# A state space stage: running sums of the heads as rows through HBM instead of by TensorE

## The reference

```
Q = 128                                  # chunk; 256 tokens are 2 chunks
G, Hg, P, N = 4, 8, 64, 128              # 4 groups of 8 heads, head width 64, state width 128
dt = softplus(dt_raw + dt_bias)
cs = cumsum(dt * A, axis=positions of the chunk)          # one running sum per head and chunk
xdt = xs * dt
seg = cs[i] - cs[j]                                       # i, j positions of one chunk
decay = exp(where(i >= j, seg, -inf))
CB = einsum("ign,jgn->ijg", Cm, Bm)
y_diag = einsum("ijgh,jghp->ighp", CB * decay, xdt)
states = einsum("jgn,jgh,jghp->ghpn", Bm, exp(cs[last] - cs), xdt)
y_off = einsum("ign,ghpn,igh->ighp", Cm, state of the chunk before, exp(cs))
y = y_diag + y_off + xs * D_skip
out = rmsnorm(y * silu(z)) @ out_w
```

## Time and profile before

| what | value |
|---|---|
| median of three runs | 3217.51 us |
| the profiled execution | 3220.12 us, its span 3218.3 us |
| PE busy | 3141.3 us (98%) |
| VectorE busy | 1262.0 us (39%) |
| ScalarE busy | 704.8 us (22%) |
| GpSimd busy | 278.2 us (9%) |
| chain that ended last | PE 84%, DMA 9%, VectorE 4% |
| granted clock of the whole span | 0.993 |
| the stage of the change | slots 0 to 31, about 48 to 203 us |

### The profile page before, as it was taken

The page is one execution under the profiler, slowest core; times in us unless marked ns, Lnnn a source line. Parts: engine busy times, 40 slices in busy tenths (PEclk is TensorE's granted clock), DMA queues, the critical chain, the costliest instruction groups (busy, mean ns, idle before and its releaser), DMA issues.

```text
span 3218.3 us, 44517 instructions
## 1 busy us (share of the span) xinstructions
PE 3141.3 (98%) x18164; PEld 2444.3 (76%) x18164; DVE 1262.0 (39%) x2669; ACT 704.8 (22%) x1251; POOL 278.2 (9%) x231
## 2 busy tenths in 40 slices
PE   8999999998999999999999999999999999999998
PEld 7888899987899888998789988888554455545444
DVE  4532177463378544753357543431211111111111
ACT  3531121252221043102211123420111111111111
POOL 0120011061011110001100013200000000000000
PEclk9999999999999999999999999999999999999999
DMA  5233244432344433443244433235799999999996
GB/s 226 105 131 131 101 174 164 164 131 92 118 159 160 157 126 119 171 171 144 105 153 170 171 144 130 75 127 209 318 428 428 428 428 428 429 428 429 428 429 260
DMA packets 71250, 715.30 MB, mean 222 GB/s; under 512 B 7969, under 2 KB 7969, under 8 KB 9153
## 3 DMA queue, kind: packets, MB, share of 16 engines
q1 hardware_dynamic: 70416, 710.06, 55.9%
q0 software_dynamic: 688, 3.15, 0.3%
HBM read 712.13 MB, written 1.05 MB: 222 GB/s over the span
## 4 chain that ended last, share of the span: by engine, by line
PE 84%; DMA 9%; DVE 4%; ACT 1%; issue 1%; POOL 0%; SPq 0%; DVEq 0%; POOLq 0%; ACTq 0%
PE bank L285 30%; PE bank L2375 11%; PE bank L3448 10%; DMA weight_ring<-in_experts 9%; PE bank L304 8%; PE bank L1374 8%; PE bank L3479 5%; PE bank L3433 2%; PE bank L3425 2%; PE bank L2673 1%; DVE residual L1119 1%; PE bank L1226 0%; PE bank L1206 0%; PE bank L344 0%; PE bank L758 0%
## 5 line engine op out<-in xcount | busy, mean ns | idle before, releaser
L285 PE MATMUL bank<-normed_residual,weight_ring 128*128 128x256 f32 x2592 | 576.1, 380 | 0.0
L285 PEld LDWEIGHTS bank<-normed_residual,weight_ring 128*128 128x128 f32 x2592 | 487.7, 190 | 71.8 <-issue 8.5
L285 PE MATMUL bank<-arena,weight_ring 128*128 128x256 f32 x1368 | 304.2, 383 | 4.7 <-ACT arena L1733 3.9
L285 PEld LDWEIGHTS bank<-arena,weight_ring 128*128 128x128 f32 x1368 | 262.0, 192 | 41.8 <-issue 4.8
L3532 DVE TENSOR_TENSOR arena<-bank,arena 128x512 f32<-128x512 f32 x32 | 22.1, 691 | 615.9 <-PE bank L3448 615.9
L3448 PE MATMUL bank<-weight_ring,arena 128*64 128x512 f32 x1024 | 227.6, 593 | 3.1 <-DMA weight_ring<-in_experts 3.1
L3448 PE MATMUL bank<-arena 128*64 128x512 f32 x1024 | 226.9, 596 | 2.3 <-DVE arena L3526 2.3
L304 PE MATMUL bank<-gained_residual,weight_ring 128*128 128x256 f32 x896 | 205.7, 390 | 23.9 <-DVE gained_residual L378 12.0
L3479 PE MATMUL bank<-weight_ring,arena 128*64 128x512 f32 x992 | 219.7, 595 | 0.0
L304 PEld LDWEIGHTS bank<-gained_residual,weight_ring 128*128 128x128 f32 x896 | 174.9, 196 | 51.4 <-DVE gained_residual L378 14.0
L3448 PEld LDWEIGHTS bank<-weight_ring,arena 128*64 128x64 f32 x1024 | 72.6, 137 | 152.7 <-issue 139.0
(11 more groups left out here) (446 smaller groups left out, 4253.9 us busy)
## 6 DMA issues: line engine op xcount, KB each, us to landing
weight_ring<-in_stream SPq DMA_DIRECT2D x290, 1024.0 KB, 4.8
weight_ring<-in_experts SPq DMA_DIRECT2D x126, 2048.0 KB, 18.6
arena<-in_experts SPq DMA_DIRECT2D x66, 2048.0 KB, 18.7
residual<-in_x SPq DMA_DIRECT2D x1, 1024.0 KB, 4.9
arena<-in_mem POOLq DMA_DIRECT2D x1, 1024.0 KB, 5.3
out<-gained_residual SPq DMA_DIRECT2D x4, 256.0 KB, 2.8
constants<-in_con SPq DMA_DIRECT2D x1, 612.5 KB, 7.3
vectors<-in_vec SPq DMA_DIRECT2D x1, 548.5 KB, 6.2
```

The source lines that it names most:

```text
L285: mm = nc.tensor.matmul(PB[b][:, m * T:m * T + T], l, r, start=(kc == 0), stop=(kc == chunks - 1))
```

## The change

The running sums of all 32 heads as rows are made once: two more matmuls in front of slot 0, with DTA as the weights and `upto` moving, give 32 partitions (one per head) by 128 positions for each chunk, in bank 4. ScalarE copies them to the arena (`CS_ROWS`). GpSimd issues a DMA that writes them to a scratch tensor in HBM (32 KB), waits for it, and then issues loads that read the rows of four heads and both chunks, 4 KB, into each of the 128 partitions, 512 KB per load. There are eight such loads, one per pair of batches, into two buffers in turn: two at once, each later one after the L1017 of the pair that used the buffer. VectorE's subtraction and ScalarE's ECS read these buffers instead of banks 4 and 5. L758 is gone with its waits, and the head outputs go to banks 4 and 5, so bank 6 holds states alone. The wait for the states moves to the head outputs of chunk 1, for their own group.

A few semaphores of later blocks are merged (`lam_in` and `lb_ready` into `exp_in`, `lam_exp` and `lbs` into `exp_out`), with the counts of the waits adapted; they make no difference in what waits for what.

```diff
+        CS_ROWS = A[0:32, 72, :]
+        def seg_rows(n):
+            return flat(92 + 4 * (n % 2), 4).rearrange("p (c t) -> p c t", c=2)
+        def seg_source(i):
+            return seg_rows(i // 2)[:, i % 2, :]
         def y_bank(j):
-            return PB[7 - j % 2]
+            return PB[4 + j % 2]
@@ ssm_slot_pe
             if s in CR_AT:
-                pe.wait_ge(sem["dte_in"], 1)
-                if i >= 2:
-                    pe.wait_ge(sem["seg_ready"], i - 1)
-                if i >= 3:
-                    pe.wait_ge(sem["ecs_ready"], (i - 1) // 2)
-                for k in range(4):
-                    h = g * HPG + half * 4 + k
-                    mm = nc.tensor.matmul(PB[4 + i % 2][:, k * P:k * P + P], DTA[:, c, h:h + 1].broadcast_to([P, P]),
-                                          upto, start=True, stop=True)
-                mm.then_inc(sem["cr_mm"], 1)
                 if i % 4 == 0:
                     pe.wait_ge(sem["xde_ready"], g + 1)
...
                     if g:
-                        pe.wait_ge(sem["y_ready"], 4 * g - 2)
+                        pe.wait_ge(sem["st_ready"], g)
@@ head outputs
-                pe.wait_ge(sem["st_ready"], before(CR_AT[0:16:4], s + 1))
                 if c:
+                    pe.wait_ge(sem["st_ready"], g + 1)
                     pe.wait_ge(sem["cp_ready"], j // 2 + 1)
@@ ssm_pe, in front of slot 0
+            for c in range(2):
+                mm = nc.tensor.matmul(PB[4][0:32, c * P:c * P + P], DTA[:, c, :], upto, start=True, stop=True)
+            mm.then_inc(sem["cs_mm"], 1)
@@ ssm_act, after silu_act(act, 2)
+            act.wait_ge(sem["cs_mm"], 1)
+            nc.scalar.activation(CS_ROWS, PB[4][0:32, 0:T], ACT.Identity)
@@ ssm_slot_act
-                    nc.scalar.activation(flat(ECS, 2), PB[4 + i % 2][:, :], ACT.Exp).then_inc(sem["ecs_ready"], 1)
+                    nc.scalar.activation(flat(ECS, 2), seg_source(i), ACT.Exp).then_inc(sem["ecs_ready"], 1)
@@ ssm_slot_dve
-                dve.wait_ge(sem["cr_mm"], i + 1)
+                if c == 0:
+                    dve.wait_ge(sem[f"seg_in{i // 2 % 2}"], 16 * (i // 4 + 1))
@@ ssm_pool
+        def rows_pool(pool, n):
+            src = io["rows"][:, 4 * n:4 * n + 4, :].rearrange("c h t -> c (h t)").unsqueeze(0).broadcast_to([P, 2, 512])
+            pool.dma_start(seg_rows(n), src).then_inc(sem[f"seg_in{n % 2}"], 16)
...
             pool.wait_ge(sem["dte_ready"], 1)
+            pool.dma_start(io["rows"].rearrange("c h t -> h c t"),
+                           CS_ROWS.rearrange("h (c t) -> h c t", c=2)).then_inc(sem["cs_sent"], 16)
+            pool.wait_ge(sem["cs_sent"], 16)
+            for n in range(2):
+                rows_pool(pool, n)
...
+                    if n + 2 < 8:
+                        rows_pool(pool, n + 2)
```

More of the change, by code:

```diff
@@ L182 @@
 cb_mm cbm_ready btok_ready dte_in dte_ready xt_mm xdt_ready xde_ready st_mm st_ready
-cr_mm seg_ready ecs_ready e_ready g_ready cp_ready y_mm y_ready
+cs_sent seg_in0 seg_in1 seg_ready ecs_ready e_ready g_ready cp_ready y_mm y_ready
 sc_mm s_read smax_ready exp_done p_ready pt_mm pts_ready o_mm o_evac
@@ L187 @@
 z_mm zabs_ready zln_ready spm_ready rs_mm rs_read sw_ready so_mm so_evac
-lam_in lam_mm lam_exp lam_ready
+exp_in lam_mm exp_out lam_ready
 hn_sq hn_stat hn_var hn_std hn_out
 kf_ready b_ready d_ready lev_exp q_side k_side lev_mm lev_taken ho_mm ho_evac oa_ready
-lb_ready lbs hg_sig hg_fg sq_q
+hg_sig hg_fg sq_q
 rt_mm rt_log rt_exp wt_ready up_act up_taken dn_taken tr_mm x_done out_written
@@ L803, in ssm_pe @@
                 nc.tensor.matmul(PB[5][:, c * 32:c * 32 + 32], upto, DTA[:, c, :], start=True, stop=True)
-            nc.tensor.matmul(PB[5][:, 64:96], ones, DTA[:, 0, :], start=True, stop=True).then_inc(sem["cs_mm"], 1)
+            nc.tensor.matmul(PB[5][:, 64:96], ones, DTA[:, 0, :], start=True, stop=True)
+            for c in range(2):
+                mm = nc.tensor.matmul(PB[4][0:32, c * P:c * P + P], DTA[:, c, :], upto, start=True, stop=True)
+            mm.then_inc(sem["cs_mm"], 1)
             for s in range(32):
@@ L923, in ssm_slot_dve @@
                     ins = nc.vector.tensor_scalar(flat(SEG + 2 * (i % 2), 2)[:, k * P:k * P + P],
-                                                  PB[4 + i % 2][:, k * P:k * P + P], CS[:, c, h:h + 1], 0.0,
+                                                  seg_source(i)[:, k * P:k * P + P], CS[:, c, h:h + 1], 0.0,
                                                   ALU.subtract, ALU.min)
@@ L1483, in ffn_pe @@
             if l:
-                pe.wait_ge(sem["lam_in"], 1)
+                pe.wait_ge(sem["exp_in"], 1)
                 nc.tensor.matmul(PB[6][:, 0:8], ones, LAMP, start=True, stop=True).then_inc(sem["lam_mm"], 1)
@@ L1489, in ffn_pe @@
                     if l and n == 1:
-                        pe.wait_ge(sem["lam_exp"], 1)
+                        pe.wait_ge(sem["exp_out"], 1)
                     ffn_block_pe(pe, l, n)
@@ L1509, in ffn_act @@
                 act.wait_ge(sem["lam_mm"], 1)
-                nc.scalar.activation(LAME, PB[6][:, 0:8], ACT.Exp).then_inc(sem["lam_exp"], 1)
+                nc.scalar.activation(LAME, PB[6][:, 0:8], ACT.Exp).then_inc(sem["exp_out"], 1)
             for p in range(23):
@@ L1569, in ffn_dve @@
                                                   ALU.mult)
-                ins.then_inc(sem["lam_in"], 1)
+                ins.then_inc(sem["exp_in"], 1)
             ffn_sums_dve(dve, own, l, 0)
@@ L1615, in ffn_dve @@
                     tables_dve(dve, own, "pos2", vec("inv2", 0))
-                    dve.wait_ge(sem["lam_exp"], 1)
+                    dve.wait_ge(sem["exp_out"], 1)
                     own(nc.vector.tensor_tensor(LAM, LAME[:, 0:4], LAME[:, 4:8], ALU.subtract))
@@ L2476, in mlp_act @@
                 tables_act(act, 1)
-                act.wait_ge(sem["lb_ready"], 1)
-                nc.scalar.activation(SC[:, 32:48], SC[:, 32:48], ACT.Exp).then_inc(sem["lbs"], 1)
+                act.wait_ge(sem["exp_in"], 2)
+                nc.scalar.activation(SC[:, 32:48], SC[:, 32:48], ACT.Exp).then_inc(sem["exp_out"], 1)
             squares_act(act, f"ple{l}", lambda e, p: wait_block(e, l, "x", p))
@@ L2621, in bounds_dve @@
                 ins = nc.vector.tensor_tensor(SC[:, 32 + 8 * k:40 + 8 * k], vec("hg_lb", 8 * k, 8), MX, ALU.subtract)
-            ins.then_inc(sem["lb_ready"], 1)
-            dve.wait_ge(sem["lbs"], 1)
+            ins.then_inc(sem["exp_in"], 1)
+            dve.wait_ge(sem["exp_out"], 2)
             own(nc.vector.tensor_tensor(LBS, LBA, LBB, ALU.add))
@@ L3805 @@
         io[k] = nc.dram_tensor(f"in_{k}", v.shape, mybir.dt.from_np(v.dtype), kind="ExternalInput").ap()
+    io["rows"] = nc.dram_tensor("rows", (2, 32, P), F32, kind="Internal").ap()
     io["out"] = nc.dram_tensor("out_0", (P, DC, T), F32, kind="ExternalOutput").ap()
```

## The result

The changed kernel takes 3201.93 us (median of four runs, 3200.58 to 3203.91) against 3218.03 of the kernel before in the same comparison (four runs, 3216.74 to 3218.67). The ratio is 0.9949, with a 95% interval of 0.9937 to 0.9961: 16.1 us, half a percent, faster. The forecast was 3202, range 3197 to 3210.

A forecast was written before the change was run, and what follows sets the result against it. TensorE was taken to set the pace. Terms -15.3 + 0.9 + 0.45 - 5.0 + 3.6 gave -15.3 us: 3220.1 profiled to 3204.8, with the run median 2.6 lower, so 3202; range 3197 to 3210.

The forecast's parts named there:

- the new wait: Before the state matmul L767 in two slots, TensorE waits for GpSimd's XDE: 1.8 us each, 3.6 in all.
- L758 out of PE's stream: Removing 16 batches of four running-sum matmuls from TensorE's stream in the state space stage saves 15.3 us.
- seams: Where head outputs now directly follow a half projection, each costs 0.10 us more; nine places, 0.9 us.
- L806: Two added 128-column matmuls before slot 0 cost 0.45 us, bounds 0.4 and 0.5; ScalarE's copy is covered, cost 0.
- waits on states: TensorE's three waits for ScalarE's copy of the states, 5.0 us together, all go.
- The rows: Eight 512 KB row loads land in 4 to 5 us, before VectorE needs them; cost 0.
- Rival 1, the ports: GpSimd stands aside twice for VectorE's SBUF subtractions at each of two places; 4.5 us come back, 3207; chance 0.20.
- Rival 2: XDE comes in time, so TensorE has no new wait: -18.9, giving 3198.6 us; chance 0.15.
- rival 4: Work goes but the kernel's end doesn't move, as a later stretch waits for something else: 3217.5 us; chance 0.07.

The follow-up runs named there:

- experiment 4: Changed kernel with XDE of groups 2 and 3 put before GpSimd's ECS product and row load of the pair before: 3199.31 us, ratio 0.9941.
- experiment 2: Kernel before, computing running sums only for batches 0 and 1, the other 14 left out: 3208.15 us, ratio 0.9969.
- experiment 1: Kernel before, with head outputs of chunk 0 no longer waiting for the copy of the states: 3215.24 us, ratio 0.9990.
- experiment 3: Changed kernel with GpSimd's row loads 3, 5 and 7 issued behind the next group's XDE instead of in front: 3201.79 us, ratio 0.9948.
- Experiment 7: Changed kernel with each row load from pair 2 on issued one pair later, right before it is needed: 3219.85 us, ratio 1.0006.
- experiment 6: Changed kernel with the eight row loads reading all-different 2 KB pieces of the weights in HBM, same size and destination: 3204.35 us, one run.
- experiment 5: Changed kernel with the old wait put back, every head output waiting for all states multiplied so far: 3207.89 us, ratio 0.9965.

## Why the prediction was right, step by step

The forecast of the time was right to a tenth of a microsecond, which is luck: the sum for the stage was -15.3 and the stage moved by -16.4, since the new wait came out 1.25 us below its forecast and the other terms balance only 0.2 of that; and the median of the kernel before was 3218.03 in this comparison, 0.5 above the one that I started from.

The measured column goes from start to start of PE's rows, as the forecast did for L758. An idle row is a little shorter than what its wait costs: L781 follows L767 after 0.95 us where nothing waits (experiment 4), and followed it after 2.80, 2.63 and 2.62 before.

| step | forecast, us | measured, us |
|---|---|---|
| L758 out of PE's stream | -15.3 | consistent with -15.3 (experiment 2) |
| seams | +0.9 | +1.1 |
| L806 | +0.45 | +0.64 |
| waits on states | -5.0 | -5.2 (5.0 in the idle rows) |
| new wait on XDE, twice | +3.6 | +2.35, by experiment 4 (1.9 in the idle rows) |
| stage | -15.3 | -16.4 |

- **L758.** Experiment 2 took 14 of the 16 batches away and got 9.4 us, 11.0 at the full clock. Its terms are -13.4 for the batches and +1.2 for seams, as I had put them, and from its rows +1.8 for XDE and -0.7 for waits on states that changed: -11.1. Sized right.
- **Seams.** The size of each, 0.10, was right and the count was not. L758 stood in front of L781 at eleven places; nine have a half projection in front, and at the two others the transposes pay too (0.97 us up to L781 where it was 0.88 up to L758).
- **L806.** Three small matmuls took 0.59 us; with L806 it is 1.23 (47.57 to 48.80). Two matmuls of 128 columns cost 0.64 and not half of four, 0.14 above my upper bound. ScalarE's copy took 0.36 us and was covered, as said.
- **The waits on states.** The reason was right, but it was two edits, and the larger part of it (3.3 of 5.0, experiment 1) comes from the wait alone. That bank 6 forced all three, as the forecast had it, is wrong: heads of chunk 0 never used bank 6.
- **The new wait.** The place, the cause and the count were right; the size was 1.8 each and is 1.1. PE came 5.6 us after the start of the transposes, as forecast; L767 started at 6.7 and not at 7.4. The step that was mis-sized is the chain behind the transposes. Four subtractions from SBUF take 0.86 instead of the 1.13 of the bank (I had put 1.1), XDE takes 1.05 instead of 1.49 because the issue moved it behind VectorE's L968, L767 follows XDE after 0.10 and not 0.25, and the issue took 0.74, not 0.58. Experiment 2 shows the chain by itself, experiment 3 the part of the issue, and experiment 4 takes the wait away.
- **The rows.** "4 to 5 us" of landing was mis-sized: 6.7, up to 8.7. Pair 4, named as the tightest, was issued at 120.75, landed 7.0 us later and was read at 130.41, so 2.7 us were left of the 3 or 4 that I believed, and it cost nothing. The later pairs did not have the 10 or more that I gave them: pairs 5 and 7 were read 9.5 us after their issue (129.89 to 139.38 and 150.72 to 160.22), with as little to spare. The 8.7 is pair 1, which is read 29 us after it lands. Experiment 7 shows what lies beyond.
- **Rival 1, the ports.** The mutual blocking is there, but in the changed kernel it falls on VectorE. In three of the 16 batches a GpSimd operation starts within the four subtractions, and they take 1.96 to 1.98 us instead of 0.86; the whole of it is one subtraction, the longest of this row (ns, min, median, max), and VectorE has the room:

```profile
L929 DVE TENSOR_SCALAR arena<-arena,small x64: 273/279/1393, 76.3 to 164.5; 128x128 f32<-128x128 f32 x64
```

  Every issue of a row load took 0.70 to 0.75, the first two beside an idle VectorE too. The trap that the Trainium skill describes ("SBUF — State Buffer", SBUF: two separate sides), a GpSimd DMA whose descriptors wait for VectorE, shows in none of the eight; but none stood beside L929 for more than 0.33 us, so a long instruction of that kind was not tried. The same section says that whoever starts first holds the ports for the whole instruction and the other fully blocks. The full block agrees: the held subtraction (130.41, 1.39 us) ends 0.1 after XDE does. Who gets them is not plain here, as its row starts 0.25 before XDE's.
- **Rival 2** (no new wait) and **rival 4** (the end doesn't move) are out by the profile.

## What to carry to other kernels

Work taken out of the stream of the engine that bounds the stage pays in full only as far as the other engines' chains to its next matmul are shorter than what is left in front of it. Add up that chain from the first thing it hangs on, and put its last link as early in its engine's program as its inputs allow. A wait that names the newest of several results where an older one would do costs as much as real work; look at which buffer each reader uses before giving anything a bank of its own. A transfer that lands before it is needed is free, and one that is on the path is paid at each turn of the buffers, so state its margin in numbers, for each transfer by itself.

## What the runs showed of the hardware that I had not expected

- Reading the same 4 KB of HBM into all 128 partitions took 6.7 us from issue to landing (5.3 to 8.7). Another 512 KB, from distinct addresses and another tensor, took 4.8 (4.6 to 6.0, experiment 6).
- Four 128x128 fp32 subtractions took 0.86 us from SBUF where they took 1.13 from a PSUM bank, but 1.28 (experiment 4) to 1.98 when a GpSimd operation ran beside them. From the bank no four of them met GpSimd in the kernel before; in experiment 2 they did, and took 1.11.
- In experiments 2 and 7, idle gaps of PE of 2.67 us and of 3.2 to 4.3 us were followed by stretches at the lower of the two levels of its clock (0.50 from 116 to 118 us in experiment 2, and from 130 to 132 and 184 to 186 in experiment 7). The gap of 2.43 us in experiment 5 and that of 1.78 before were not.
